# Weight loads moved to another issuing engine and placed behind key blocks, in a one-layer decoder step

## What is computed

```python
h = _rms(x, g_pre)
z = h @ w_in                       # 1024 -> 7 x 512: u, v_A, gate_A, q, k, v, gate_B
ya = gelu(ua) * (tril(W_s) @ rms_group(gelu(va)) + b_s)
yb = attend(q, k, v)               # 8 heads of 64
y  = concat(rms(ya) * silu(ga), rms(yb) * silu(gb)) @ w_out
x + _rms(y, g_post)
```

## Time and profile before

| what | us |
|---|---|
| median of three runs | 443.77 |
| these runs, lowest to highest | 442.79 to 444.88 |
| the profiled execution | 447.82 |
| its span, first to last instruction | 446.2 |

### The profile page before, as it was taken

One profiled execution on the slowest core, in us unless ns is written; L12 is line 12 of the kernel. 1 busy time (PEld: TensorE's weight loads), 2 busy tenths in 40 slices (PEclk: granted clock), 3 DMA queues, 4 the chain that ended last, 5 costly groups with the idle time before them and its releaser, 6 DMA issues. The chain is left out here.

```text
span 446.2 us, 9123 instructions
## 1 busy us (share of the span) xinstructions
PE 396.1 (89%) x2770; PEld 192.2 (43%) x2770; DVE 258.6 (58%) x685; ACT 123.6 (28%) x278; POOL 280.1 (63%) x440
## 2 busy tenths in 40 slices
PE   5796999998999899987999799988999899999433
PEld 3552355344533454433644554444344453344332
DVE  1174286447833696567674787586445497378410
ACT  3310120000214265453742386524231001100101
POOL 5777655585758466777569467875468566767500
PEclk9998999999999999998999899999899899999658
DMA  8999359997899759994988569939999649935400
GB/s 261 400 380 386 84 198 373 321 273 267 273 355 331 221 172 340 312 283 146 301 279 227 166 194 335 285 110 346 374 330 294 190 136 346 308 86 137 147 2 3
DMA packets 78559, 111.22 MB, mean 249 GB/s; under 512 B 45832, under 2 KB 46984, under 8 KB 78512
## 3 DMA queue, kind: packets, MB, share of 16 engines
q0 software_dynamic: 22576, 71.45, 46.9%
q1 hardware_dynamic: 45296, 23.97, 20.4%
q10 hardware_dynamic: 10640, 15.24, 10.9%
HBM read 106.31 MB, written 4.29 MB: 248 GB/s over the span
## 5 line engine op out<-in xcount | busy, mean ns | idle before, releaser
L1072 PE MATMUL PA<-wbuf,hT 128*128 128x512 f32 x384 | 183.8, 620 | 0.0
L904 POOL DMA_INDIRECT K<-in_cache_k,kidx x128 | 133.2, 1040 | 75.7 <-issue 36.7
L726 DVE TENSOR_TENSOR ksum<-K 128x512 f32<-128x512 f32 x128 | 85.2, 689 | 48.6 <-DMA K<-in_cache_k,kidx 29.7
L1072 PEld LDWEIGHTS PA<-wbuf,hT 128*128 128x128 f32 x384 | 70.8, 196 | 77.7 <-issue 76.9
L710 POOL DMA_DIRECT2D V<-in_cache_v x128 | 76.2, 597 | 14.8 <-issue 10.1
L1181 PE MATMUL PA<-wbuf,hT 128*128 128x512 f32 x128 | 58.5, 603 | 0.1
L739 POOL TENSOR_TENSOR ksum<-K,qb 128x128 f32<-128x128 f32 x64 | 29.8, 498 | 23.7 <-DVE selT L1609 18.3
L739 DVE TENSOR_TENSOR ksum<-K,qb 128x128 f32<-128x128 f32 x128 | 38.4, 369 | 3.8 <-DVE selT L1609 3.5
L1197 PE MATMUL GB<-ksum,win 128*32 128x512 f32 x256 | 35.2, 622 | 2.5 <-DVE ksum L726 2.5
L1181 PEld LDWEIGHTS PA<-wbuf,hT 128*128 128x128 f32 x128 | 23.5, 192 | 28.6 <-issue 28.2
L919 POOL TENSOR_SCALAR rstd<-msum 128x1 f32<-128x1 f32 (+1 forms) x24 | 8.1, 339 | 36.5 <-ACT junk L1272 11.2
(11 more groups left out here) (211 smaller groups left out, 379.6 us busy)
## 6 DMA issues: line engine op xcount, KB each, us to landing
wbuf<-in_w_in ACTq DMA_DIRECT2D x5, 2048.0 KB, 12.5
V<-in_cache_v SPq DMA_DIRECT2D x240, 32.0 KB
V<-in_cache_v POOLq DMA_DIRECT2D x128, 32.0 KB, 6.3
wbuf<-in_w_out ACTq DMA_DIRECT2D x2, 2048.0 KB, 13.6
wbuf<-in_w_in SPq DMA_DIRECT2D x4, 512.0 KB, 8.0
wbuf<-in_w_in SPq DMA_DIRECT2D x1, 2048.0 KB, 21.3
K<-in_cache_k,kidx POOLq DMA_INDIRECT x128, 7.7
qb<-q_rows SPq DMA_DIRECT2D x8, 256.0 KB, 3.9
```

The costliest lines, as they stand in the source:

```text
L726: eng.tensor_tensor(ksum[:, n % SUMS, :], K[:, at, 0, :], K[:, at, 1, :], ALU.add).then_inc(s_dsum, 1)
L904: pool.indirect_dma_start(K[:, m % SLOTS, :, :].rearrange("p r w -> p (r w)"), None, k_rows, bass.IndirectOffsetOnAxis(ap=kidx[:, b, n:n + ...
L1072: last = pe.matmul(bank[:, :], lhs, rhs, start=(kc == 0), stop=(kc == KC - 1))
```

## The change

Weight loads w2 to w8 leave from SP instead of ACT. In the plan, SP gets a lane of its own for them, ahead of all its others, with a step `wl`; it waits for the last tile of chunk c and for the last key block of a named sequence (w2 for sequence 0, w3 for sequence 1, and so on to w8 for sequence 6). The transfer of a weight is reckoned at 7.0 us instead of 9.0, and values count as landed 2.5 us after their transfer instead of 0.8. ACT's step for chunk q goes.

```diff
+LOAD_BEHIND = {2: 0, 3: 1, 4: 2, 5: 3, 6: 4, 7: 5, 8: 6}
...
-                       ("DVE", "first " + DVE_LANES), ("POOL", POOL_LANES), ("SP", "spread rows residual fetch gather"),
+                       ("DVE", "first " + DVE_LANES), ("POOL", POOL_LANES), ("SP", "weights spread rows residual fetch gather"),
...
             if t == NT - 1 and c + 2 < len(CHUNKS) + 2:
-                if name == "q":
-                    add("ACT", "evacuate", ("pj", c, t), 0.5, ("PE", ("pj", c, t)))
-                add("Q", "weight", ("w", c + 2), 9.0, ("ACT", ("pj", c, t)))
+                add("SP", "weights", ("wl", c + 2), 0.8, ("PE", ("pj", c, t)), ("Q", ("k", LOAD_BEHIND[c + 2], NB - 1)))
+                add("Q", "weight", ("w", c + 2), 7.0, ("SP", ("wl", c + 2)))
...
-        ends[eng, s] = clock[eng] + {"Q": 0.8}.get(eng, 0.0)
+        ends[eng, s] = clock[eng] + (0.0 if eng != "Q" else 2.5 if s[0] == "v" else 0.8)
...
+                elif kind == "wl":
+                    c = s[1]
+                    pa_full_wait(sp, ("pj", c - 2, NT - 1))
+                    sp.wait_ge(s_k[NB - 1], 16 * (LOAD_BEHIND[c] + 1))
+                    sp.dma_start(wbuf[:, c % 2, :, :], w_src(c)).then_inc(s_w[c % 2], 16)
...
-                if kind == "pj" and s[2] == NT - 1 and s[1] + 2 < WCH:
-
-                    c = s[1] + 2
-                    pa_full_wait(act, s)
-                    act.dma_start(wbuf[:, c % 2, :, :], w_src(c)).then_inc(s_w[c % 2], 16)
...
-                    if name == "q":
-                        continue
```

More of the change, by code:

```diff
@@ L616, in hymba_kernel @@
         gate_b = [gain[:, :], wsT[:, :, :].rearrange("p g t -> p (g t)"), vn[:, 0, :], vn[:, 1, :]]
-        WCH = len(CHUNKS) + 2
         krow_t = [yb[:, t, :] for t in range(NT)]
```

## The result

| | before | after |
|---|---|---|
| median of the runs, us | 444.32 (442.79 to 447.24) | 429.38 (426.80 to 432.80) |
| the profiled execution, us | 447.82 | 426.80 |
| its span, us | 446.2 | 425.2 |

The changed kernel takes 0.9654 of the time before, 95% interval 0.9597 to 0.971: 15.4 us less, 2.1 times the 7.3 us forecast. The direction was right, 429.38 lies just inside the range, and the size was wrong. The profiled executions lie further apart (21.0 us of span) than the medians (14.9), because before's lies above all of its four runs and after's is the lowest of its four.

A forecast was written before the change was run, and what follows sets the result against it. TensorE, busy 396.1 of 446.2 us, was taken as the bound, losing most to value waits. 9.0 us gained less 1.7 for w2 gives 7.3, from the median 443.77 to 436.5 us; range 429 to 447.

The forecast's parts named there:

- Value waits and clock drops: TensorE before pv steps: 14.2 us of waits fall to 4.2, two of three clock drops go; 13.5 us in all.
- 10.1 counted: The part of TensorE's 14.2 us of waits for value rows that was forecast to go.
- 9.0 us: What of the 13.5 us saved on TensorE was forecast to reach the last gate and so the end.
- Part 2: Weight loads moving from ACT's queue to SP's: counted as nothing, except a 1.7 us loss for w2.
- 1.7 us wait for w2: TensorE waits for w2, landing after 12.2 us, because the planner can put its first reader 2 us sooner.
- The tail behind it as long as now: A sign of being right: last gate some 7 us earlier, with the work behind it taking as long as before.
- cap of 2.1 us a gate: TensorE comes about 2.1 us late behind the key sums, so each gate can gain no more than that.
- w4, w5 and w8 issued 8 to 16 us later and landing in 12 us or less: A sign of being right: these three weight loads leave SP behind the keys and land faster.
- (b): Rival: TensorE reaches gates sooner but stands for key sums, with 1.7 us clock drops; 442 to 446 us, chance 0.13.
- (c): Rival: a weight load on SP's queue delays the value fetch behind it, pv steps wait; 443.5 us, chance 0.09.
- (d): Rival: w4 leaves SP late and TensorE stands 5 to 12 us for it; 443 to 450 us, chance 0.16.

The follow-up runs named there:

- e3: The kernel before, with values reckoned as landed 2.5 us after their transfer instead of 0.8 and nothing else changed; ratio 0.9941.
- e2: The changed kernel with a weight reckoned at 9.0 us again, so moved loads and later values only; ratio 0.9705 to the kernel before.
- e6: The changed kernel's order, but ACT issues all weight loads except w3, without a wait for keys; ratio 0.9834 to the kernel before.
- e4: The changed kernel, same order, without SP's run-time wait for the last key block; ratio 0.9706 to the kernel before.
- e12: The kernel before, same order, with the weight loads put by hand into SP's row behind the keys; ratio 0.9942.
- e9: The changed kernel with both planner numbers put back (weight 9.0, values 0.8), so only the loads moved; ratio 0.9879 to the kernel before.
- e1: The kernel before, with a weight reckoned at 7.0 us instead of 9.0 and nothing else changed; ratio 1.0069.
- e8: The kernel before with both planner numbers changed (weight 7.0, values 2.5), ACT still issuing the weights; ratio 1.0007.
- e13: e6 with w4 held back on ACT until about the moment the changed kernel sends it; ratio 0.9789 to the kernel before.
- e7: As e12, but with SP's step for w8 placed behind a value fetch; ratio 1.0218 to the kernel before.

## Why the prediction was wrong in size

**Value waits and clock drops: right.** They fell to 3.5 us (fewer than 6 were forecast), and the one low-clock slice that is left on the way to the last gate follows a wait for DVE. e3 shows the first half alone: V from 14.2 to 6.5 us, which is 7.7 of the 10.1 counted. What the sum left out is that other waits come up where these go: in after the idle time ahead of the gate fell by 5.4 us, not by the 11.5 by which the value waits ahead of it did. The drops were counted by the length of an idle, and e3 shows that length alone does not decide (last section).

**"9.0 us" for what reaches the end: the term was too large by itself.** e3 measured 2.6 us (0.4 to 4.8). Its profiled span is 10.0 us shorter, but that execution is the lowest of its ten, set against one of before's highest. The prediction read its 14.2 us of waits from that high execution and took their removal from the median; that the waits of a median run are shorter is only argued.

**Part 2, "I count nothing for it": the step that failed.** The moved loads measured 5.4 us (3.0 to 7.8) alone, 10.5 us on top of the later values (e3 to e2), and 6 to 8 in after's own order (e6 against e4 and after). The prediction had the loads compete with keys alone, and ruled the gain out because TensorE and not the keys was late. Two things were missing. First, it did not ask what weights beside the values do to the values, on which TensorE did wait: in e12, with the old order, V falls from 14.2 to 8.1 us, and 2.6 us reach the end. It had that contention in hand: the earlier trace rows shows all three together at a DMA share of 1.07. Nor did the reason hold for the keys in the new order: e6 has 8.0 us of key-sum waits, after 2.5. Second, it priced the loads in the old order, while the planner made another with a fuller tail: in e9 most of the idle time saved is there (21.1 to 16.6 us).

**The 1.7 us wait for w2: right mechanism, wrong queue.** It is in e1 (1.68), e6 (1.6), e8 (1.8) and e13 (1.7), all with w2 on ACT's queue. On SP's, w2 lands in some 8 us, not the 12.2 that the prediction carried over, and the wait is gone.

**"The tail behind it as long as now": wrong.** The last gate came 27.5 us earlier and the tail grew by 6.5. The sum took the old order with gaps closed; the planner made a new one that holds projection work back for the tail. The cap of 2.1 us a gate, 12.6 for six gates, was a property of the old order too.

**"w4, w5 and w8 issued 8 to 16 us later and landing in 12 us or less": half right.** w4 left 14.3 us later, w5 5.3 and w8 0.7 (7.6 and 10.1 in e12, which keeps the old order). w5 landed in 8.4 us; the view of after has no landing for w4 and w8, and in e4, with after's order, they took 9.1 and 18.7.

**The rivals.** (b) did not come for key sums, 2.5 us of waits; its mechanism came for DVE's `mx`, 4.2 us, one of them with a drop of the clock. (c) may have its mechanism, 18.03 us for a fetch that took 13.36 before, though over all kernels these times overlap; for that fetch its price is 0, the lower end given for it, as those values have slack. (d) did not come for w4, which left at 147.76, but e7 shows that it is there, 11.66 us, if a load stands one fetch too late in SP's row.

**Open.** Why later values and moved loads give 13.1 us together and 8.0 as a sum of their parts is only argued: each alone leaves waits long enough to hold up the next gate. By the idle column the surplus lies ahead of the gate (9.5 us less in e2, 4.5 and 1.7 less in e3 and e9), not in the tail. Where the queue's 4 us come from is shown for w2's 1.7 only: that POOL's and SP's transfers gain from there being two queues instead of three fits the waits of e13, but no run measured it transfer by transfer, and w4, w6, w7 and w8 land in about the same time from either queue.

## What to carry to other kernels

Where several queues run at the limit, the queue on which a large load goes can decide who waits for it (here about 4 us of 444): try it ahead of work with slack on the same queue, and off the path of what the bound engine waits for. In a kernel with a planned order, each reckoned time moves everything; cost an edit against the order that the planner will make, idle time ahead of the last gate and behind it apart, and measure the edits in pairs, since here two were worth 2.6 and 5.4 us alone and 13.1 together. Compare medians before taking a gap in one profile for the gain.

## What was not expected of the hardware

The same 2 MB, sent at nearly the same moment (62 to 64 us), lands in 12.2 us from ACT's queue and in 8.4 from SP's; sent at 147 to 149 us it lands in 9.2 and 9.1. The granted clock halved for 3.4 us after a TensorE idle of 2.39 us in after, as it had after 2.35 us in before, while the five value waits of up to 0.88 us in after were followed by no drop. The length of an idle does not decide it alone: in e3 one of 2.71 us, longer than both, was followed by no drop. A window of after, then the wait and a window of e3 (the third number from the end is PEclk):

```profile
298.50:301.90 3.40, 3.40 (x15) 1.77 (x12) 1.40 (x5) 0.00 (x0) 2.93 (x4) 0.50 1.03 397
```

```profile
349.13 0.21 PE L1222 MATMUL DC<-psm,one 128*32 128x2 f32 x5 [2.71 <-DMA V<-in_cache_v]
```

```profile
349.10:352.50 3.40, 3.37 (x62) 2.06 (x63) 3.26 (x10) 0.21 (x1) 2.13 (x3) 1.00 0.31 66
```
